# A two-layer encoder trunk on one core: x loaded by channel, an activation-table load moved to the loop's head, and the last additions cut in halves

## What is computed

```python
def rms_norm(x, g):
    y = x * lax.rsqrt(jnp.mean(x * x, axis=-1, keepdims=True) + RMS_EPS)
    return y * g
def fourier_mixer(h, w_in, w_out):            # w_in, w_out: 1024 x 1024
    u = (h @ w_in).reshape(B, S, 4, 256)
    return jnp.fft.fft2(u, axes=(1, 3), norm="ortho").real.reshape(B, S, D) @ w_out
def swiglu(h, w_gate, w_up, w_down):          # dense: 2816 wide; expert: 3584 wide, 8 experts
    return (jax.nn.silu(h @ w_gate) * (h @ w_up)) @ w_down
for i in range(2):
    h = h + mix(rms_norm(h, norm_mix[i]))
    h = h + feed_forward(rms_norm(h, norm_ffn[i]))   # layer 1: each token's two experts, weighted
return rms_norm(h, final_norm)
```

## Time and profile before

| | |
|---|---|
| median of three runs | 1378.86 us (1378.75 to 1379.13) |
| the profiled execution | 1379.58 us, span 1377.8 us, granted clock 0.993 |
| PE busy | 1349.4 us, 98% of the span |
| PEld / DVE / ACT / POOL busy | 1120.4 / 1111.5 / 920.1 / 33.8 us |
| DMA | 431.27 MB, mean 313 GB/s |

### The profile page before, as it was taken

How to read it: one execution, slowest core, us unless ns; L and a number is a source line. 1 busy time by engine, 2 the same in 40 slices (tenths; PEclk the granted TensorE clock), 3 DMA queues, 4 the chain that set the end, 5 groups by cost and what they waited for, 6 DMA issues and landing times.

```text
span 1377.8 us, 17441 instructions
## 1 busy us (share of the span) xinstructions
PE 1349.4 (98%) x6369; PEld 1120.4 (81%) x6369; DVE 1111.5 (81%) x811; ACT 920.1 (67%) x747; POOL 33.8 (2%) x48
## 2 busy tenths in 40 slices
PE   9999999999999999999999999999999999999997
PEld 7888888787877887888788788888878888888775
DVE  5756666655678888888988888898888889889987
ACT  6554444445647777777777777777777777777674
POOL 0000000000110000000000000000000000002000
PEclk9999999999989999999999999999999999999999
DMA  9666775462339999999999999999999999999992
GB/s 347 218 206 181 216 214 191 163 204 92 113 125 372 374 378 362 394 372 364 392 372 370 369 391 372 370 383 366 384 367 392 369 368 388 373 377 381 394 362 93
DMA packets 194940, 431.27 MB, mean 313 GB/s; under 512 B 19601, under 2 KB 22033, under 8 KB 194897
## 3 DMA queue, kind: packets, MB, share of 16 engines
q1 hardware_dynamic: 178752, 415.66, 82.8%
q0 software_dynamic: 3360, 11.78, 2.2%
q10 hardware_dynamic: 12784, 3.26, 1.7%
HBM read 424.89 MB, written 5.78 MB: 313 GB/s over the span
## 4 chain that ended last, share of the span: by engine, by line
PE 89%; DVE 5%; ACT 3%; issue 2%; DMA 0%; ACTq 0%; POOL 0%; DVEq 0%
PE bank_G L1248 10%; PE bank_G L1250 10%; PE bank_G L1249 10%; PE bank_U L1248 9%; PE bank_U L1250 9%; PE bank_U L1249 9%; PE bank_Y L1248 8%; PE bank_Y L1250 8%; PE bank_Y L1249 8%; DVE w_lo L752 2%; PE bank_T L1689 2%; ACT w_hi L454 1%; PE bank_T L1248 1%; PE bank_T L1250 1%; PE bank_T L1249 1%
## 5 line engine op out<-in xcount | busy, mean ns | idle before, releaser
L752 DVE TENSOR_TENSOR w_lo<-raw,w_hi 128x2048 fp32r<-128x2048 f32 x390 | 885.8, 2289 | 195.2 <-ACT w_hi L454 195.1
L454 ACT ACTIVATE w_hi<-raw 128x2048 fp32r<-128x2048 f32 x390 | 747.0, 1919 | 286.7 <-PE bank_U L1250 91.1
L1248 PE MATMUL bank_Y<-w_hi,hidT_hi 128*128 128x512 f32 x492 | 192.3, 391 | 0.0
L1250 PE MATMUL bank_Y<-w_hi,hidT_lo 128*128 128x512 f32 x492 | 191.6, 390 | 0.0
L1249 PE MATMUL bank_Y<-w_lo,hidT_hi 128*128 128x512 f32 x492 | 191.5, 389 | 0.0
L1248 PE MATMUL bank_G<-w_hi,xg_hi 128*128 128x512 f32 x448 | 175.6, 392 | 11.0 <-DVE w_lo L752 10.0
L1248 PE MATMUL bank_U<-w_hi,xg_hi 128*128 128x512 f32 x448 | 179.1, 400 | 0.0
L1250 PE MATMUL bank_U<-w_hi,xg_lo 128*128 128x512 f32 x448 | 175.0, 391 | 0.0
L1250 PE MATMUL bank_G<-w_hi,xg_lo 128*128 128x512 f32 x448 | 174.5, 390 | 0.0
L1249 PE MATMUL bank_U<-w_lo,xg_hi 128*128 128x512 f32 x448 | 174.5, 390 | 0.0
L1249 PE MATMUL bank_G<-w_lo,xg_hi 128*128 128x512 f32 x448 | 174.4, 389 | 0.0
(11 more groups left out here) (302 smaller groups left out, 1366.6 us busy)
## 6 DMA issues: line engine op xcount, KB each, us to landing
raw<-in_expert_w_gate SPq DMA_DIRECT2D x112, 1024.0 KB, 7.4
raw<-in_expert_w_up SPq DMA_DIRECT2D x112, 1024.0 KB, 7.5
raw<-in_expert_w_down SPq DMA_DIRECT2D x112, 1024.0 KB, 7.4
raw<-in_nat_w_qkv SPq DMA_DIRECT2D x12, 1024.0 KB, 5.1
raw<-in_ffn_w_gate SPq DMA_DIRECT2D x11, 1024.0 KB, 8.9
raw<-in_ffn_w_up SPq DMA_DIRECT2D x11, 1024.0 KB, 6.0
raw<-in_ffn_w_down SPq DMA_DIRECT2D x11, 1024.0 KB, 5.1
raw<-in_fourier_w_out SPq DMA_DIRECT2D x4, 1024.0 KB, 15.9
```

What stands on the lines that cost most here:

```text
L454: nc.scalar.activation(w_hi[w][:], raw[s][:], ACT.Copy).then_inc(hi_made, 1)
L752: nc.vector.tensor_tensor(w_lo[w][:], raw[s][:], w_hi[w][:].bitcast(f32), ALU.subtract).then_inc(lo_made, 1)
L1248: nc.tensor.matmul(out_, xh, wh, start=start, stop=False)
L1250: return nc.tensor.matmul(out_, xl, wh, start=False, stop=stop)
```

## The change

1. The host lays out x also by channel (`x_cols`, 128 x 8 x 256). The 16 transposes of x are gone; ACT and DVE split `x_cols` from SBUF. The first projection (`first_projection`) does both token blocks for each part of a piece. ACT's queue issues `gains` and the first two quarters of `x_cols`, SP's the rest of it behind the four parts of piece 0; `x_turns` (now one load, for the squares only) comes behind piece 2, `ident`, `h` and `mask` behind piece 5. Twelve idle matmuls in place of 10 + 8.
2. On ACT each expert begins with a Silu of one column (`silu_first`), and the split of piece 3 moves from the end of a pass to behind it. DVE's order in the loop is not changed.
3. Each addition of fetched rows is cut into column halves, one after `hidden` of a step, one at the next down piece, over steps 2 to 5. `add_result` and the branch for overfull experts wait for all eight.

```diff
-        for c in range(2):
-            cs = slice(BANK * c, BANK * (c + 1))
-            sp.dma_start(fo["x_turns"][:, :, cs], x[0, :, cs].rearrange("(p b) d -> p b d", b=NB)).then_inc(s_x[c], 16)
-            first_piece(2 * c)
-            first_piece(2 * c + 1)
+        for part in range(PARTS):
+            first_piece(part)
+        sp.dma_start(fo["x_cols"][:, 4:], x_cols_c[:, 4:]).then_inc(s_x[2], 16)
         for j, (src, tiles, _) in enumerate(dense):
             if j:
                 load(j, None, src, tiles)
+            if j == 2:
+                sp.dma_start(fo["x_turns"][:], x[0].rearrange("(p b) d -> p b d", b=NB)).then_inc(s_turns, 16)
             if j == 3:
                 sp.dma_start(fo["dft_raw"][:], dft_c.rearrange("(b p) n -> p b n", p=P)).then_inc(s_dft, 16)
+            if j == 5:
+                sp.dma_start(ident[:], ident_c).then_inc(s_ident, 16)
                 sp.dma_start(h[:], x[0].rearrange("(b p) d -> p b d", p=P)).then_inc(s_h, 16)
+                sp.dma_start(mask[:], mask_c).then_inc(s_mask, 16)
...
-        act.dma_start(ident[:], ident_c).then_inc(s_ident, 16)
         act.dma_start(gains[:], gains_c).then_inc(s_gains, 16)
-        act.dma_start(mask[:], mask_c).then_inc(s_mask, 16)
+        for n in range(2):
+            act.dma_start(fo["x_cols"][:, 2 * n:2 * n + 2], x_cols_c[:, 2 * n:2 * n + 2]).then_inc(s_x[n], 16)
...
         def expert(E, ahead, kept=True):
 
+            nc.scalar.activation(mo["silu_first"][:], half_power[:, 0:1], ACT.Silu)
             for j, (kind, c, half) in enumerate(EXPERT):
-                if j < AHEAD - SPLIT:
-                    continue
...
-            if ahead:
-                for j in range(PER_EXPERT + SPLIT, PER_EXPERT + AHEAD):
-                    split_hi(j, E)
...
-        def add_terms(n):
+        def add_term(n, b, q):
 
-            for b in range(NB):
-                dve.wait_ge(s_terms, 16 * 2 * NB)
-                if n:
-                    dve.wait_ge(terms_added, b + 1)
-                nc.vector.scalar_tensor_tensor(out=h[:, b], in0=mo[("hn_hi", "hn_lo")[n]][:, b].bitcast(f32),
...
+            cs = slice(BANK * q, BANK * (q + 1))
+            dve.wait_ge(s_terms, 16 * 2 * NB)
+            if n:
+                dve.wait_ge(terms_added, 2 * b + q + 1)
+            nc.vector.scalar_tensor_tensor(out=h[:, b, cs], in0=mo[("hn_hi", "hn_lo")[n]][:, b, cs].bitcast(f32),
...
-                    elif c == 2:
-                        add_terms(0)
-                    elif c == 3:
-                        add_terms(1)
+                    elif 2 <= c < 6:
+                        add_term((c - 2) // 2, c % 2, 0)
...
+                if (kind, half) == ("down", 0) and kept and not sweep and 1 <= c < 5:
+                    add_term((c - 1) // 2, (c - 1) % 2, 1)
...
+        def first_projection():
+
+            for n, j in enumerate(FIRST_PIECES):
+                wh, wl = parts(j, None, PARTS)
+                for k in range(PARTS):
+                    kk = PARTS * n + k
+                    pe.wait_ge(act_lo_done, kk // 2 + 1)
...
+                    for b in range(NB):
+                        last = three(G[b][:], act_hi[:, kk, P * b:P * (b + 1)], act_lo[:, kk, P * b:P * (b + 1)],
+                                     wh[:, k], wl[:, k], kk == 0, kk == KD - 1)
...
-        still(10)
+        still(12)
+        first_projection()
+        project(at["w_in"][1], U, BANK, u_psum)
         pe.wait_ge(s_ident, 16)
-        transpose_stream(0, 0)
-        still(8)
-        project(at["w_in"][0], G, BANK, u_psum, stream_second(0))
-        project(at["w_in"][1], U, BANK, u_psum)
         pe.wait_ge(dft_lo_done, 1)
```

More of the change, by code:

```diff
@@ L202, in trunk @@
     arena_start = nc.sbuf_base
-    mo_more = [("y_row", [P, D], f32), ("place", [P, 2, NB], f32), ("past", [P, 2, NB], f32), ("source", [P, 2, NB], u32)]
+    mo_more = [("y_row", [P, D], f32), ("place", [P, 2, NB], f32), ("past", [P, 2, NB], f32), ("source", [P, 2, NB], u32), ("silu_first", [P, 1], f32)]
     moe_l += mo_more
@@ L243, in trunk @@
     s_bias = [sem(f"s_bias{step}") for step in range(BIAS_STEPS)]
-    s_x = [sem(f"s_x{c}") for c in range(2)]
+    s_x = [sem(f"s_x{n}") for n in ("_cols0", "_cols1", "_cols2")]
+    s_turns = sem("s_turns")
     s_first = [sem(f"s_first{part}") for part in range(3)]
@@ L495, in stream_hi @@
             for q in (2 * half + n for n in quarters):
-                act.wait_ge(tr_done, 4 * i + q + 1)
+                if i:
+                    act.wait_ge(tr_done, 4 * (i - 1) + q + 1)
+                else:
+                    act.wait_ge(s_x[min(q, 2)], 16)
                 for k in range(2):
-                    last = nc.scalar.activation(act_hi[:, 2 * q + k], two(STREAM[i][q])[:, k], ACT.Copy,
+                    source = two(STREAM[i][q])[:, k] if i else fo["x_cols"][:, 2 * q + k]
+                    last = nc.scalar.activation(act_hi[:, 2 * q + k], source, ACT.Copy,
                                                 scale=gains[:, i, 2 * q + k:2 * q + k + 1])
                 last.then_inc(act_hi_done, 1)
-        act.dma_start(ident[:], ident_c).then_inc(s_ident, 16)
         act.dma_start(gains[:], gains_c).then_inc(s_gains, 16)
-        act.dma_start(mask[:], mask_c).then_inc(s_mask, 16)
+        for n in range(2):
+            act.dma_start(fo["x_cols"][:, 2 * n:2 * n + 2], x_cols_c[:, 2 * n:2 * n + 2]).then_inc(s_x[n], 16)
         act.wait_ge(rstd_chain, 1)
@@ L730, in _ @@
             gather_hi(NE + 1)
-            for j in range(PER_EXPERT, PER_EXPERT + AHEAD):
+            for j in range(PER_EXPERT, PER_EXPERT + SPLIT):
                 split_hi(j, LAST)
@@ L784, in stream_lo @@
                     kk = 2 * q + k
-                    last = rest_scaled(act_lo[:, kk], two(STREAM[i][q])[:, k], gains[:, i, kk:kk + 1], act_hi[:, kk])
+                    source = two(STREAM[i][q])[:, k] if i else fo["x_cols"][:, kk]
+                    last = rest_scaled(act_lo[:, kk], source, gains[:, i, kk:kk + 1], act_hi[:, kk])
                 last.then_inc(act_lo_done, 1)
@@ L1256, in project @@
                 tiles = PIECE // width
-                if j not in FIRST_PIECES:
-                    ready(j, None)
+                ready(j, None)
                 wh, wl = parts(j, None, tiles)
@@ L1274, in project @@
                 last.then_inc(piece_used, 1)
+        def first_projection():
[4 more added lines that the diff above has]
+                    pe.wait_ge(act_lo_done, kk // 2 + 1)
+                    if k < PARTS - 1:
+                        pe.wait_ge(lo_part, (PARTS - 1) * BY_PARTS.index(j) + k + 1)
+                    else:
+                        ready(j, None)
+                    for b in range(NB):
+                        last = three(G[b][:], act_hi[:, kk, P * b:P * (b + 1)], act_lo[:, kk, P * b:P * (b + 1)],
+                                     wh[:, k], wl[:, k], kk == 0, kk == KD - 1)
+                        if kk == KD - 1 and b < NB - 1:
+                            last.then_inc(u_psum, 1)
+                last.then_inc(piece_used, 1)
         def transpose_stream(i, half):
-            if i == 0:
-                pe.wait_ge(s_x[half], 16)
-            else:
-                pe.wait_ge(h_half, 2 * (i - 1) + half + 1)
+            pe.wait_ge(h_half, 2 * (i - 1) + half + 1)
             for q in (2 * half, 2 * half + 1):
@@ L1286, in transpose_stream @@
                         kk = 2 * q + k
-                        of = h if i else fo["x_turns"]
-                        last = nc.tensor.transpose(STREAM[i][q][:, o:o + P], of[:, b, P * kk:P * (kk + 1)], ident[:])
+                        last = nc.tensor.transpose(STREAM[i][q][:, o:o + P], h[:, b, P * kk:P * (kk + 1)], ident[:])
                 last.then_inc(tr_done, 1)
@@ L1300, in before @@
             def before(n, b):
[L1301 removed]
+                if (n, b) == (0, 0):
                     pe.wait_ge(act_lo_done, 4 * i + 2)
@@ L1818 @@
     gains = np.stack([inputs["norm_mix"], inputs["norm_ffn"]], 1).reshape(4, KD, P).transpose(2, 0, 1)
-    for name, a in [(n, inputs[n]) for n in _INS] + [("gains", gains), ("slide", slide)] + list(shape_constants().items()):
+    x_cols = np.asarray(inputs["x"][0]).reshape(P, NB, KD, P).transpose(3, 2, 1, 0).reshape(P, KD, S)
+    for name, a in [(n, inputs[n]) for n in _INS] + [("x_cols", x_cols), ("gains", gains), ("slide", slide)] + list(shape_constants().items()):
         a = np.ascontiguousarray(a)
```

28 lines of the change are left out of this document (9 added, 19 removed).

## The result

The changed kernel takes 1366.97 us (median of 4 runs, 1366.76 to 1367.15) and the kernel before, beside it, 1378.80 us (1378.04 to 1379.13): ratio 0.9915, 95% interval 0.9898 to 0.9932, so 11.8 us faster. The forecast was 1366.7. The profiled execution of the changed kernel took 1367.15 us with a span of 1365.3, against 1379.58 and 1377.8 before.

A forecast was written before the change was run, and what follows sets the result against it. PE holds 89% of the chain, so time is won only where PE waits or loses work. Heads 8.2 + additions 3.3 + start 0.7 = 12.2 us off 1378.86 gives 1366.7 us; 8-in-10 range 1363.0 to 1372.5.

The forecast's parts named there:

- Head of a pass: Start of each of seven passes: early table load and later piece 3 split remove PE's wait, 1.17 us each, 8.2 us.
- The fit: At a pass head, piece 3's rest ready at 532.6, PE needing it by 532.8: it fits by 0.2 us.
- rival 1: Pass head: the loop's branch delays the table load, so the loop saves only 2.5 us, 1372.4 us in all; 8%.
- Rival 2: Pass head: the table load brings a 1.38 us drain, each pass 0.15 us worse, 1376.0 us in all; 4%.
- rival 3: Pass head: branch and drain together make PE wait for piece 3's rest in up 0, 1382.2 us, slower than before; 3%.
- Additions: Last expert: halved additions remove two PE waits, 3.7 us, less 0.1 in each of four steps: 3.3 us kept.
- Rival 5: Last expert: the halves don't fit, each of four steps waits 0.5 us, 1368.5 us; no separate chance, inside the forecast's range.
- Start: Kernel start: PE loses 16 transposes, third Fourier step at about 35.3 instead of 35.77; 0.7 us, bounds 0 and 3.0.
- `w_out` chain: Kernel start: late `w_out` load, its splits, `u_lo` twice and `pt_lo` hold PE's third Fourier step to about 35.3.
- Rival 4: Kernel start: the `w_out` piece isn't what ends last, so the 2 to 3 us stay, 1364.5 us; 15%.
- The clock in the router's stage: Router's stage: TensorE's half-clock stretch may end sooner or later against the gathers; 1.5 us allowed both ways, outside the sum.

The follow-up runs named there:

- e4: The whole change with `still(20)` in place of `still(12)`, so 40 unread products at the start in place of 24; measured 1366.75 us.
- e5: The delay run: the whole change with ten more one-column Silus ahead of piece 3's split at each head; measured 1370.93 us.

## Why the prediction was right, step by step

- **Head of a pass: right.** 1.17 us times seven was the term; the passes took 8.35 us less (1.19 each), and 8.48 alone. Each event of the step was there: load at the end of a split, small Silu, split of piece 3, silu without a load, no wait at gate 1. The pass takes 118.7 us where 118.8 was said. The fit was said to be 0.2 us; the delay run gives 0.23. More room was said to be in the first pass, and there the delay cost nothing. What I chose for the unknown, that the load may follow the loop's branch at once, is what the trace shows, 0.02 us behind the split; rival 1 (2.5 us for the loop) is out.
- **The drain: none.** By the rule of the Trainium skill ("ScalarE: Activation LUTs", What ACT_TABLE_LOAD costs) each load would bring 1.38 us more. No row here shows it: 0.02 us ahead of the load and 0.01 behind it at the loop head, both with the move and without. Rival 2 and, with it, rival 3 fall. By rival 2's own numbers such a drain would have cost the whole term and 1.1 us more, not "nearly all" of it.
- **Additions: the mechanism right, the size off by 0.4 us.** I took 3.7 less four times 0.1; it was 3.7 less four times 0.21, 2.9 us, inside the bounds of 1.8 to 3.7. The step that was mis-sized is the second half's place, "0.1 us short of what the piece after it needs". Rival 5, 0.5 us for each of four steps, is the same mechanism at more than twice the price.
- **Start: right on average, for a reason half seen.** 0.7 us was the term and 0.7 is the mean of six executions against four. The `w_out` chain does end last when the clock is high (e4, 34.6 us, and e5), and in two of the three kernels at 0.72. I had 35.3, since I let its split start at 29.01 as before; 29.01 + 6.21 is 35.2, so that the chain was right, but the split starts at 27.95 to 28.89. What I missed is that the change itself opens a pause of 3 us ahead of the first product, and that a low clock afterwards can make PE's own projection the last to end: in the first profile after, PE starts the Fourier stage at 33.28, before at 33.44, and the forecast's reason doesn't hold there. The first product was said to come near 7.5 us and came at 8.65; that the mean gain is 0.7 nonetheless is in part luck, since PE's own way was last in three of the six executions and the chain began earlier than I said in the other three. The third step was forecast "no earlier than 34" and was never earlier than 34.17. Rival 4, the start in full, is out.
- **The clock in the router's stage: the allowance was right and was used.** 1.5 us both ways was allowed; the executions differ by 1.2 us there, and the first profile after happened to have a short low stretch. That cancelled what its start had lost, which is luck: the forecast's total fits this one execution better than its terms do.
- **The sum.** 8.4 + 2.9 + 0.7 = 12.0 us against 12.2 forecast and 11.8 between the medians. In the one profiled execution it is 8.35 + 2.90 + 0.16 + 1.09 = 12.5, of which 1.1 belong to no part of the change. Without the repeated runs this would have read as a start that pays 1.25 us.

## What to carry to other kernels

A table load can be moved into an engine's idle time by a one-column activation of the same function, but look at what queues behind it: two thirds of the gain here came from the early load, the rest from moving the next split behind it, and 0.23 us more in that place would have been the end of the slack. A work item that delays a critical one by less than the list of waits shows still costs: read the period of a step (17.01 against 16.80 us), and put the item where its engine waits. Where a change takes PE's first work away or shortens it, look at what PE does in the pause, and judge stretches of some microseconds by several executions, not by one.
